# Hybrid attention trunk in float32: softmax scaled before the transposes, values stationary in column halves, scores in pairs

## The reference

```
h = RMSNorm(x); columns of h @ w_in -> A (u, v), B (q, k, v), C (3 parts), D (latents), 4 gates of width 1024
A: chunked causal gMLP gating          C: gated width-3 convolution
B: causal attention, 4 heads of 64      D: latent attention, 4 heads, q/k of 96 (64 + 32 rotary), v of 64
  s = q k^T * scale, masked; p = softmax(s); out[q, :] = sum_k p[q, k] v[k, :]
merged = sum_i sigmoid(gate_i) * (branch_i @ w_branch[i]);  x += RMSNorm(merged @ w_out)
x += RMSNorm(relu(RMSNorm(x) @ w_mlp_in)^2 @ w_mlp_out)
```

## Time and profile before

| what | value |
|---|---|
| median of 3 runs | 828.12 us (827.99 to 829.35) |
| profiled execution | 828.51 us |
| its span, first to last instruction | 826.7 us |
| mean granted TensorE clock | 0.994 |
| PE busy | 808.6 us, 98% of the span |
| PEld / DVE / ACT / POOL busy | 705.8 / 483.7 / 405.8 / 58.2 us |
| HBM read | 144.83 MB, 176 GB/s over the span |

### The profile page before, as it was taken

One profiled execution on the slowest core, in us unless ns is written; L12 is line 12 of the kernel. 1 busy time (PEld: TensorE's weight loads), 2 busy tenths in 40 slices (PEclk: granted clock), 3 DMA queues, 4 the chain that ended last, 5 costly groups with the idle time before them and its releaser, 6 DMA issues.

```text
span 826.7 us, 13275 instructions
## 1 busy us (share of the span) xinstructions
PE 808.6 (98%) x4670; PEld 705.8 (85%) x4670; DVE 483.7 (59%) x627; ACT 405.8 (49%) x623; POOL 58.2 (7%) x89
## 2 busy tenths in 40 slices
PE   6999999999999999999989999999999999999997
PEld 6898788887899999999878977888878999999995
DVE  4488444449776555555374784445597765555543
ACT  4565555443455444444254655554435644444432
POOL 2010000006110000000010100000061000000000
PEclk9999999999999999999999999999999999999999
DMA  7687444564467565565347865445645575655531
GB/s 235 199 271 219 151 154 151 155 204 153 128 188 227 178 195 180 177 203 180 127 118 217 276 185 151 150 143 169 201 129 157 175 229 179 202 189 179 190 127 52
DMA packets 85436, 146.58 MB, mean 177 GB/s; under 512 B 4965, under 2 KB 50421, under 8 KB 85381
## 3 DMA queue, kind: packets, MB, share of 16 engines
q1 hardware_dynamic: 85188, 145.32, 56.0%
q0 software_dynamic: 192, 0.57, 0.2%
HBM read 144.83 MB, written 1.05 MB: 176 GB/s over the span
## 4 chain that ended last, share of the span: by engine, by line
PE 93%; issue 2%; DVE 2%; DMA 1%; POOL 1%; ACT 1%; DVEq 0%; SPq 0%; ACTq 0%; POOLq 0%
PE banks L1095 29%; PE banks L1096 28%; PE banks L1097 28%; DMA raw<-in_w_in_dram 1%; PE banks L1165 1%; PE banks L1107 1%; PE banks L1173 1%; PE banks L1164 1%; PE banks L1115 1%; DVE gate_th L898 0%; PE banks L1233 0%; PE banks L1190 0%; PE banks L1189 0%; PE banks L1245 0%; POOL rstd L1053 0%
## 5 line engine op out<-in xcount | busy, mean ns | idle before, releaser
L685 DVE TENSOR_TENSOR w_lo<-raw,w_hi 128x1024 fp32r<-128x1024 f32 (+1 forms) x272 | 316.1, 1198 | 153.2 <-ACT w_hi L427 151.9
L427 ACT CAST w_hi<-raw 128x1024 fp32r<-128x1024 f32 (+1 forms) x272 | 264.5, 1013 | 156.1 <-PE banks L1097 114.2
L1095 PE MATMUL banks<-w_hi,xT_hi 128*128 128x512 f32 (+2 forms) x480 | 182.7, 381 | 3.0 <-DVE xT_lo L704 3.0
L1096 PE MATMUL banks<-w_lo,xT_hi 128*128 128x512 f32 (+2 forms) x480 | 178.9, 373 | 0.0
L1097 PE MATMUL banks<-w_hi,xT_lo 128*128 128x512 f32 (+2 forms) x480 | 178.9, 373 | 0.0
L1095 PE MATMUL banks<-xT_hi,w_hi 128*128 128x256 f32 x576 | 164.0, 285 | 0.0
L1097 PE MATMUL banks<-xT_hi,w_lo 128*128 128x256 f32 x576 | 163.0, 283 | 0.0
L1096 PE MATMUL banks<-xT_lo,w_hi 128*128 128x256 f32 x576 | 163.0, 283 | 0.0
L1095 PE MATMUL banks<-w_hi,brT_hi 128*128 128x512 f32 x320 | 125.0, 391 | 0.0
L1096 PE MATMUL banks<-w_lo,brT_hi 128*128 128x512 f32 x320 | 124.8, 390 | 0.0
L1097 PE MATMUL banks<-w_hi,brT_lo 128*128 128x512 f32 x320 | 124.5, 389 | 0.0
(11 more groups left out here) (170 smaller groups left out, 534.4 us busy)
## 6 DMA issues: line engine op xcount, KB each, us to landing
raw<-in_w_in_dram SPq DMA_DIRECT2D x96, 512.0 KB, 4.6
raw<-in_w_mlp_in_dram SPq DMA_DIRECT2D x64, 512.0 KB, 4.3
raw<-in_w_mlp_out_dram SPq DMA_DIRECT2D x64, 512.0 KB, 4.3
raw<-in_w_branch_dram SPq DMA_DIRECT2D x16, 512.0 KB, 4.1
raw<-in_w_out_dram SPq DMA_DIRECT2D x16, 512.0 KB, 4.0
raw<-in_w_in_dram SPq DMA_DIRECT2D x16, 176.0 KB, 2.4
gain_pre<-in_g_pre_mix_dram SPq DMA_DIRECT2D x2, 512.0 KB, 5.7
gain_pre<-in_g_pre_mlp_dram SPq DMA_DIRECT2D x2, 512.0 KB, 6.1
```

Source lines behind the costliest of these rows:

```text
L427: nc.scalar.copy(w_hi[:, c % RING, h * n:(h + 1) * n], raw[:, q % RAW, 0:n]).then_inc(hi_ready, 1)
L685: v.tensor_tensor(w_lo[:, c % RING, cut], raw[:, q % RAW, 0:n], w_hi[:, c % RING, cut].bitcast(F32), ALU.subtract).then_inc(lo_ready, 1)
L1095: nc.tensor.matmul(dst, l_hi, r_hi, start=first, stop=False)
L1096: nc.tensor.matmul(dst, l_hi, r_lo, start=False, stop=False)
```

## The change

The probabilities are divided by their row sums before they are transposed: a reciprocal and two `tensor_scalar` per head on DVE, after `head_exp`. The value product is turned round: v (64 columns) is stationary, the transposed probabilities move, and the two heads of a pair write to partitions 0 to 63 and 64 to 127 of one bank. The result stands with the features on partitions already, so the scaling of the result, `o_sb` and the four transposes per branch are gone, and the split into `brT_hi` and `brT_lo` reads the bank directly, in steps 19 and 23. Scores are issued two heads at a time, after chunks 13, 15, 17 and 19, behind the transposes instead of ahead of them; in B the two heads lie on rows 0 to 63 and 64 to 127 of the array. Values are issued in pairs after chunks 16, 18, 20 and 22.

```diff
--- before.py
+++ after.py
@@ -125,7 +125,6 @@
         a_out = u_tmp
         av2 = sb("av2", [P, T, MIX])
         av_tmp = sb("av_tmp", [P, T, MIX])
-        o_sb = av_tmp
         vD = sb("vD", [P, T, HEADS * D_V])
         qTB = sb("qTB", [P, FT, S])
         kTB = sb("kTB", [P, FT, S])
@@ -235,8 +234,7 @@
         probsT_copied = sem("probsT_copied")
         attn_psum = sem("attn_psum")
         inv_sum_ready = sem("inv_sum_ready")
-        attn_ready = sem("attn_ready")
-        attnT_psum = sem("attnT_psum")
+        probs_normed = sem("probs_normed")
         brT_hi_ready = sem("brT_hi_ready")
         brT_lo_ready = sem("brT_lo_ready")
         gate_ready = sem("gate_ready")
@@ -554,10 +552,10 @@
                 if s == 16:
                     act.wait_ge(a_out_ready, nth(l, 1, 0))
                     branch_hi(l, 0, a_out)
-                if s in (20, 24):
-                    n = (s - 20) // 4
-                    act.wait_ge(attnT_psum, nth(l, 2, n))
-                    branch_hi(l, (1, 3)[n], psum[:, 4, :])
+                if s in (19, 23):
+                    n = (s - 19) // 4
+                    act.wait_ge(attn_psum, nth(l, 4, 2 * n + 1))
+                    branch_hi(l, (1, 3)[n], psum[:, (3, 5)[n], :])
                 if C_GATE < s <= C_BRANCH and (s - C_GATE) % 2 == 0:
                     gate_tanh(l, (s - C_GATE) // 2 - 1, 1)
 
@@ -750,6 +748,17 @@
                                        ALU.add, ALU.min, neg_max[:, h % 2, 0:1]).then_inc(scores_masked, 1)
                 v.tensor_tensor_reduce(probs[:, h % 2, P:3 * P], bank[:, P:3 * P], causal, scale, 3.0e38,
                                        ALU.add, ALU.min, neg_max[:, h % 2, 1:2]).then_inc(scores_masked, 1)
+
+            def head_normalise(l, h):
+
+                dve.wait_ge(probs_ready, nth(l, 16, 2 * h + 1))
+                n = h % 4
+                v.reciprocal(inv_sum[:, h // 4, :, n], row_sum[:, h // 4, :, n]).then_inc(inv_sum_ready, 1)
+                dve.wait_ge(inv_sum_ready, nth(l, 8, h))
+                for t in range(T):
+                    part = probs[:, h % 2, 0:P] if t == 0 else probs[:, h % 2, P:3 * P]
+                    v.tensor_scalar(part, part, inv_sum[:, h // 4, t, n:n + 1], None, ALU.mult
+                                    ).then_inc(probs_normed, 1)
 
             def branch_lo(l, i, order, src):
                 dve.wait_ge(brT_hi_ready, nth(l, 4, order))
@@ -858,6 +867,7 @@
                     branch_lo(l, 2, ORDER_C, conv.rearrange("p f n -> p (f n)"))
                 if 14 <= s < 22:
                     head_mask(l, s - 14)
+                    head_normalise(l, s - 14)
                 if s == 15:
                     dve.wait_ge(sv_psum, nth(l, 1, 0))
                     dve.wait_ge(u_gelu, nth(l, 1, 0))
@@ -870,20 +880,8 @@
                 if s == 16:
                     branch_lo(l, 0, ORDER_A, a_out)
                 if s in (19, 23):
-
                     n = (s - 19) // 4
-                    dve.wait_ge(probs_ready, nth(l, 16, 8 * n + 7))
-                    v.reciprocal(inv_sum[:, n], row_sum[:, n]).then_inc(inv_sum_ready, 1)
-                    dve.wait_ge(inv_sum_ready, nth(l, 2, n))
-                    dve.wait_ge(attn_psum, nth(l, 8, 4 * n + 3))
-                    four = [P, T, HEADS, HD]
-                    bank = psum[:, (3, 5)[n], :].rearrange("p (t h e) -> p t h e", t=T, h=HEADS)
-                    v.tensor_tensor(o_sb.rearrange("p t (h e) -> p t h e", h=HEADS), bank,
-                                    inv_sum[:, n].unsqueeze(3).broadcast_to(four), ALU.mult
-                                    ).then_inc(attn_ready, 1)
-                if s in (20, 24):
-                    n = (s - 20) // 4
-                    branch_lo(l, (1, 3)[n], (ORDER_B, ORDER_D)[n], psum[:, 4, :])
+                    branch_lo(l, (1, 3)[n], (ORDER_B, ORDER_D)[n], psum[:, (3, 5)[n], :])
 
             def gate_unit(l, n):
 
@@ -1147,26 +1145,29 @@
                     if t == 1:
                         last.then_inc(hiddenT_psum, 1)
 
-            def head_scores(l, h):
-                n = h % 4
-                if h < 4:
-                    part = slice(64 * (n % 2), 64 * (n % 2) + 64)
-                    q, k = qTB[part, n // 2, :], kTB[part, n // 2, :]
-                else:
-                    q, k = qTD[0:QK, n, :], kTD[0:QK, n, :]
-                if h == 0:
+            def pair_scores(l, p):
+
+                if p == 0:
                     pe.wait_ge(qkTB_copied, nth(l, 2, 1))
                     pe.wait_ge(c_out_ready, nth(l, 1, 0))
-                if h == 4:
+                if p == 2:
                     pe.wait_ge(qkTD_copied, nth(l, 4, 3))
-                if h >= 2:
-                    pe.wait_ge(scores_masked, nth(l, 16, 2 * (h - 2) + 1))
-                nc.tensor.matmul(psum[:, h % 2, 0:P], q[:, 0:P], k[:, 0:P], start=True, stop=True)
-                nc.tensor.matmul(psum[:, h % 2, P:3 * P], q[:, P:S], k, start=True, stop=True
-                                 ).then_inc(scores_psum, 1)
+                if p >= 1:
+                    pe.wait_ge(scores_masked, nth(l, 16, 4 * p - 1))
+                heads = []
+                for h in (2 * p, 2 * p + 1):
+                    n = h % 4
+                    part = slice(64 * (n % 2), 64 * (n % 2) + 64)
+                    heads.append((qTB[part, n // 2, :], kTB[part, n // 2, :]) if h < 4 else
+                                 (qTD[0:QK, n, :], kTD[0:QK, n, :]))
+                for h, (q, k) in enumerate(heads):
+                    nc.tensor.matmul(psum[:, h, 0:P], q[:, 0:P], k[:, 0:P], start=True, stop=True)
+                for h, (q, k) in enumerate(heads):
+                    nc.tensor.matmul(psum[:, h, P:3 * P], q[:, P:S], k, start=True, stop=True
+                                     ).then_inc(scores_psum, 1)
 
             def head_transpose(l, h):
-                pe.wait_ge(probs_ready, nth(l, 16, 2 * h + 1))
+                pe.wait_ge(probs_normed, nth(l, 16, 2 * h + 1))
                 if h >= 1:
                     pe.wait_ge(probsT_copied, nth(l, 8, h - 1))
                 for b in range(3):
@@ -1174,21 +1175,23 @@
                                                ident)
                 last.then_inc(probsT_psum, 1)
 
-            def head_values(l, h):
-                pe.wait_ge(probsT_copied, nth(l, 8, h))
-                if h == 0:
+            def pair_values(l, p):
+
+                pe.wait_ge(probsT_copied, nth(l, 8, 2 * p + 1))
+                if p == 0:
                     pe.wait_ge(u_gelu, nth(l, 1, 0))
-                if h == 4:
+                if p == 2:
                     pe.wait_ge(qkTD_copied, nth(l, 4, 3))
-                n = h % 4
-                v = [proj[:, t, 3 * MIX + HD * n:3 * MIX + HD * n + HD] if h < 4 else
-                     vD[:, t, D_V * n:D_V * n + D_V] for t in range(T)]
-                bank, pT = psum[:, (3, 5)[h // 4], :], probsT[:, h % 2, :]
-                nc.tensor.matmul(bank[:, HD * n:HD * n + HD], pT[:, 0:P], v[0], start=True, stop=True)
-                o = MIX + HD * n
-                nc.tensor.matmul(bank[:, o:o + HD], pT[:, P:2 * P], v[0], start=True, stop=False)
-                nc.tensor.matmul(bank[:, o:o + HD], pT[:, 2 * P:3 * P], v[1], start=False, stop=True
-                                 ).then_inc(attn_psum, 1)
+                f = p % 2
+                bank = psum[:, (3, 5)[p // 2], f * S:(f + 1) * S]
+                for t in range(T):
+                    for h in range(2):
+                        n = 2 * f + h
+                        v = (proj[:, t, 3 * MIX + HD * n:3 * MIX + HD * n + HD] if p < 2 else
+                             vD[:, t, D_V * n:D_V * n + D_V])
+                        last = nc.tensor.matmul(bank[64 * h:64 * h + 64, t * P:S], v, probsT[:, h, 2 * t * P:(2 + t) * P],
+                                                start=t == 0, stop=t == 1)
+                last.then_inc(attn_psum, 1)
 
             def side_after(l, c):
 
@@ -1256,25 +1259,12 @@
                             last = nc.tensor.matmul(psum[part, 4, o:o + P], av2[:, t, 64 * g:64 * g + 64],
                                                     w_sT[:, g, :], start=True, stop=True)
                     last.then_inc(sv_psum, 1)
-                if 13 <= c < 21:
-                    head_scores(l, c - 13)
+                if c in (16, 18, 20, 22):
+                    pair_values(l, (c - 16) // 2)
                 if 14 <= c < 22:
                     head_transpose(l, c - 14)
-                if 15 <= c < 23:
-                    head_values(l, c - 15)
-                if c in (19, 23):
-                    n = (c - 19) // 4
-                    pe.wait_ge(attn_ready, nth(l, 2, n))
-
-                    if n == 0:
-                        pe.wait_ge(a_out_ready, nth(l, 1, 0))
-                    else:
-                        pe.wait_ge(brT_lo_ready, nth(l, 4, ORDER_B))
-                    for f in range(FT):
```

(6 more changed lines are left out.)

## The result

The changed kernel takes 817.63 us (median of 4, 817.04 to 818.83) against 828.28 us of before in the same runs: ratio 0.9871, 95% interval 0.9854 to 0.9888. The profiled execution took 817.35 us, with a span of 815.5.

What follows compares the result with a forecast made beforehand. TensorE's own instruction stream bounds the kernel; result transposes 0.92, values 0.88 and scores 1.83 save 3.63 us per layer, 7.3 in two, from 828.5 to 821.2, less 0.4 for the median: 820.8 us, range 818.0 to 825.0.

Steps and rivals of the forecast that it cites:

- the cover: New division on DVE stays hidden behind TensorE: ready about 2.5 us after the chunk's start, needed at about 5.4.
- both kinds of overlap: Column halves in values and row halves in B scores run together, saving 0.88 and 1.83 us per layer; chance 0.72.
- Rivals 1 to 3: Array halves: rows don't overlap, 823.4 us (0.12); columns don't, 826.0 (0.07); neither does, 828.6 (0.04).
- Rival 4: Chain of mask, exponential, normalise, transposes no longer fits one chunk, TensorE stops before 16 transposes: 830.4 us, chance 0.03.
- 0.15 is what any block costs by interrupting the stream: Attention blocks behind chunks: fixed 0.15 us each, from chunk 23's 0.52 less some 0.37 for four transposes standing alone.
- values of one head are 0.58: Chunk 21 of before: its 1.07 us less 0.15 for interruption and 0.34 for three transposes leaves 0.58.
- the base of 5.42: Window of chunk 24, with no attention block behind it: 5.42 us; what a window has above that prices its block.
- the rule weighed ahead: Changing tiling mode drains TensorE, which speaks against the change in value blocks; no figure given, the sum used 0.33 us.
- the 0.29 of the forecast: Entry and exit of the column tiles around a pair of values: 0.29 us, within the 0.94 a pair costs.

Runs made afterwards that it cites:

- taken apart: Changed kernel with both heads of a pair on one array half: values on the lower half 823.47 us; B scores on rows 0 to 63 820.26 us.
- the scores alone: Kernel before with only the new paired scores, values and scaling of the result as before: 824.17 us, ratio 0.9956.
- The values alone: Changed kernel with the old single-head scores put back, values, scaling and result's transposes new: 822.22 us, ratio 0.9931.
- the padded kernels: Kernel before with 22, 6 or 44 increments of an unused semaphore added in VectorE's step 16: 826.24, 826.25 and 826.30 us.

## Why the prediction was right or wrong

**Right: the bound, the cover, and both kinds of overlap.** TensorE's stream was the bound, and the gain came out of its blocks. Column halves and row halves run together: taken apart they cost 5.2 us (forecast 5.2) and 2.3 us (forecast 2.6) in the windows, 5.9 and 2.6 in the time. Rivals 1 to 3 fall with that. The division is hidden: 2.4 us after the chunk's start, forecast 2.5, and nothing is gained without it. Rival 4 falls. The tanh in step 16 ended 0.27 us ahead of the second tile's first matmul at 106.61, forecast 0.3.

**Right in detail:** the scores alone saved 1.8 a layer (forecast 1.83); chunk 14 saved 0.86 (0.85), chunk 18 0.30 (0.29), chunk 20 0.29 (0.29), and chunk 22 lost 0.32 (0.36). A pair of values costs 1.00 in a block (6.79 less 5.44 less 0.35 for transposes) and 1.03 alone (6.47 less 5.44), forecast 0.94.

**Wrong step 1: "0.15 is what any block costs by interrupting the stream", and from it "values of one head are 0.58".** After the change chunk 21 has the transposes alone, and its window is 5.79, 0.35 over a chunk without a block. In a block the prediction had them at 0.34, so nothing comes on top when they stand alone. The window of before was 6.49, so the values of one head were 0.70. I had taken the 0.15 from chunk 23, whose four transposes I priced at 0.37, and out of the base of 5.42 that was read 0.02 too low. The trace of before shows what it was. Chunk 23 starts behind the values of chunk 22:

```profile
155.50 0.39 PE L1190 MATMUL banks<-vD,probsT 128*128 128x64 f32 x2
155.69 0.48 PE L1095 MATMUL banks<-w_hi,xT_hi 128*128 128x512 f32 x1
156.01 0.40 PE L1096 MATMUL banks<-w_lo,xT_hi 128*128 128x512 f32 x1
```

Its second weight matmul comes 0.32 after the first instead of 0.23, and from its first to its last (155.69 to 161.04) it takes 5.35 where chunk 25 takes 5.21. These 0.14 are left over from the block ahead; the four transposes behind the chunk add 0.36, and 0.1 more in chunk 24. In before every block leaves 0.10 to 0.14 to the next window, but a block that ends in transposes gives most of it back: the weight matmul starts 0.03 after the last transpose, where two transposes are 0.11 apart. It was therefore no price apart from the parts, and the values lost 0.12 by it, which is 1.0 us a layer for eight heads. Chunks 15, 16, 17, 19 and 21 came out 0.09, 0.06, 0.20, 0.21 and 0.12 better than forecast. Against it stand the pairs of values, dearer than forecast, and chunk 23, 0.33 instead of 0.52, of which 0.10 came back in chunk 24. The sum is 0.65 more than forecast, 4.3 a layer against 3.6, 8.6 us against 7.3. The values alone gave 4.6 us in the windows where my prices gave 3.6.

**Wrong step 2: the sum held nothing outside the windows.** The prediction named a difference from elsewhere as what would make it wrong, and 1.2 to 1.6 us are of that kind, by the ratios of the padded kernels, 0.9986 to 0.9981. Every other VectorE code run here had it, and mine counted VectorE's new instructions for their time only. With step 1 mended the forecast is 819.5, inside the range; the turn brings it to 817.9 to 818.3, the bottom end of the range. The windows and the turn make 9.8 to 10.2 us; the three measurements of the ratio, 0.9871, 0.9877 and 0.9882, are 10.7 to 9.8 us, and what is left lies within their intervals. So neither step alone takes the time out of the range; both together take it to its edge, and that the measured 817.63 lies below it and not just above is within the noise.

On the rule weighed ahead: the drain at a change of tiling (the Trainium skill, TensorEngine Tiling (Array Packing), Key Properties) fits the trace, which prices it. The values leave the last weight matmul by 0.32 instead of 0.23 and reach the transposes 0.20 after their last record. Four heads in one block, with one entry and one exit fewer, save 0.25 each time in the windows, near the 0.29 of the forecast.

## What to carry to other kernels

Where one engine is busy throughout, subtract windows that differ in one part, and test the split of an overhead on a window in which the part stands alone: what a block leaves to the next window is easily charged twice or to the wrong part. Small float32 matmuls with full stationary tiles and few moving columns are dear for what they compute (three of 64 columns cost 0.70 us here); turning them round, with the halves of the array side by side and as many as possible behind one change of tiling, paid here even with the drain: 4.6 us in the windows, with the transposes of the result that it saves. A difference of 0.1 to 0.2% between two kernels whose code differs in length can be code placement: pad the old one before explaining it.

## What the runs showed of the hardware

A loop's turn depends on an engine's code apart from its work: 4.3 to 4.4 us on VectorE against 3.2, changed alike by 6, 22 or 44 instructions that only raise an unused semaphore, and worth 1.2 to 1.6 us of 828 because TensorE had to wait for it.

A block that ends in 256-column matmuls over 96 rows hands over at a smaller loss than expected: after chunk 17 of the changed kernel the last weight product starts right behind the scores, and the next one later. Only the two together show the price.

```profile
116.41 0.61 PE L1164 MATMUL banks<-kTD,qTD 96*128 96x128 f32 x4
116.86 1.03 PE L1166 MATMUL banks<-kTD,qTD 96*128 96x256 f32 x4
117.53 0.59 PE L1093 MATMUL banks<-w_hi,xT_hi 128*128 128x512 f32 x1
117.96 0.40 PE L1094 MATMUL banks<-w_lo,xT_hi 128*128 128x512 f32 x1
```

Four records of 256 columns would be 0.86 at 0.215 each; the weight matmul starts after 0.67, and its own successor after 0.43 instead of 0.23, which gives the 0.2 back. The window of chunk 17 looks 0.2 too short and that of chunk 18 0.2 too long, so a window read by first starts can be off by that much when the block before it ends in long matmuls.
